# A diffusion backbone on one core: the next GEMM's first two tiles on scaled x, root and shift put on their results

## The reference

```
y = x * rsqrt(mean(x * x, axis=features) + 1e-6) * w
h = y * (1 + scale) + shift            # scale, shift from c (latent) or c_ctx (context)
layer 0: x += g1 * retention(h);        h2 = norm2(x); x += g2 * conv_ffn(h2)
layer 1: x += g1 * neighbourhood(h);    h2 = norm2(x); x += g2 * conv_ffn(h2)   # latent only from here
conv_ffn(h) = (silu(a) * g) @ w_down,   a, g = split(conv3(h @ w_up) + b),      hidden 2 x 2816
out = rmsnorm(x) * w
```

## Time and profile before

| | |
|---|---|
| time, median of 3 runs | 2078.77 us (2076.61 to 2079.49) |
| profiled execution | 2078.47 us, its span 2076.4 us |
| TensorE busy | 1982.3 us, 95% |
| VectorE, ScalarE, GpSimd busy | 65%, 36%, 5% |
| mean granted TensorE clock | 0.979 |
| DMA | 186.39 MB, 90 GB/s |

### The profile page before, as it was taken

How to read it: one execution, slowest core, us unless ns; L and a number is a source line. 1 busy time by engine, 2 the same in 40 slices (tenths; PEclk the granted TensorE clock), 3 DMA queues, 4 the chain that set the end, 5 groups by cost and what they waited for, 6 DMA issues and landing times.

```text
span 2076.4 us, 29858 instructions
## 1 busy us (share of the span) xinstructions
PE 1982.3 (95%) x10452; PEld 1687.3 (81%) x10452; DVE 1342.3 (65%) x2251; ACT 755.6 (36%) x1281; POOL 97.1 (5%) x162
## 2 busy tenths in 40 slices
PE   5999999999999889999999999899999889999997
PEld 4878888888888778888888887688888768788785
DVE  7866635735745677766664667777877667557375
ACT  4423223223313344312321233456556444333232
POOL 0000000000000000000000000311111000000000
PEclk8999999999999989999999999899999989999999
DMA  7221311321221112233224334211111222223222
GB/s 291 90 83 62 112 61 52 106 68 62 92 81 61 61 59 93 91 132 105 97 101 132 101 101 152 89 46 42 56 45 35 92 71 94 98 91 101 91 91 101
DMA packets 51256, 186.39 MB, mean 90 GB/s; under 512 B 5680, under 2 KB 5680, under 8 KB 51184
## 3 DMA queue, kind: packets, MB, share of 16 engines
q1 hardware_dynamic: 37744, 136.73, 19.4%
q0 software_dynamic: 13440, 48.63, 7.0%
HBM read 181.15 MB, written 4.19 MB: 89 GB/s over the span
## 4 chain that ended last, share of the span: by engine, by line
PE 83%; DVE 9%; issue 4%; ACT 3%; DMA 1%; DVEq 0%; SPq 0%; ACTq 0%
PE acc L393 58%; PE o_ps L483 3%; PE o_ps L518 3%; PE acc L606 3%; PE acc L483 2%; PE o_ps L649 2%; PE acc L664 2%; PE acc L505 2%; PE acc L448 2%; PE o_ps L664 2%; DVE pt_lo L1625 1%; PE acc L639 1%; PE o_ps L434 1%; PE acc L699 1%; DVE w_lo L1169 1%
## 5 line engine op out<-in xcount | busy, mean ns | idle before, releaser
L804 ACT ACTIVATE w_hi<-raw 128x1024 fp32r<-128x1024 f32 x232 | 245.2, 1057 | 597.5 <-PE acc L393 477.6
L1169 DVE TENSOR_TENSOR w_lo<-raw,w_hi 128x1024 fp32r<-128x1024 f32 x232 | 284.2, 1225 | 275.4 <-ACT w_hi L804 273.9
L393 PE MATMUL acc<-h_hi,w_hi 128*128 128x512 f32 x1520 | 437.5, 351 | 4.9 <-DVE w_lo L1169 3.4
L393 PE MATMUL acc<-h_hi,w_lo 128*128 128x512 f32 x1520 | 434.5, 349 | 0.0
L393 PE MATMUL acc<-h_lo,w_hi 128*128 128x512 f32 x1520 | 434.1, 349 | 0.0
L393 PEld LDWEIGHTS acc<-h_hi,w_hi 128*128 128x128 f32 x1520 | 245.2, 188 | 44.4 <-ACT u L990 4.2
L393 PEld LDWEIGHTS acc<-h_lo,w_hi 128*128 128x128 f32 x1520 | 245.0, 188 | 39.6
L393 PEld LDWEIGHTS acc<-h_hi,w_lo 128*128 128x128 f32 x1520 | 243.9, 188 | 38.7
L1336 DVE SCALAR_TENSOR_TENSOR x<-acc,mod,x 128x512 f32<-128x512 f32 (+3 forms) x136 | 81.9, 637 | 145.1 <-PE acc L393 135.7
L393 PE MATMUL acc<-act_hi,w_lo 128*128 128x512 f32 (+1 forms) x396 | 119.8, 356 | 0.0
L393 PE MATMUL acc<-act_hi,w_hi 128*128 128x512 f32 (+1 forms) x396 | 119.5, 356 | 0.0
(11 more groups left out here) (231 smaller groups left out, 3520.5 us busy)
## 6 DMA issues: line engine op xcount, KB each, us to landing
raw<-in_weights_dram SPq DMA_DIRECT2D x232, 512.0 KB, 3.3
ada_raw<-in_ada_dram POOLq DMA_DIRECT2D x80, 512.0 KB, 3.6
ada_start<-in_ada_first_dram SPq DMA_DIRECT2D x8, 1024.0 KB, 18.3
x<-in_x_in_dram SPq DMA_DIRECT2D x4, 768.0 KB, 7.0
park_dram<-x POOLq DMA_DIRECT2D x1, 2048.0 KB, 8.1
rel<-in_bias_dram POOLq DMA_DIRECT2D x16, 128.0 KB, 2.4
x<-park_dram POOLq DMA_DIRECT2D x2, 1024.0 KB, 6.6
out_dram<-x SPq DMA_DIRECT2D x8, 256.0 KB, 2.1
```

The source lines that it names most:

```text
L393: mm = nc.tensor.matmul(tile[:, c0:c0 + cn], wt[:, b * P:(b + 1) * P], mv[:, n, c0:c0 + cn], start=(n == 0 and m == 0), stop=(n == last an ...
L804: nc.scalar.activation(w_hi[i][:, :], raw[i][:, :], ACT.Copy).then_inc(hi_split, 1)
L1169: nc.vector.tensor_tensor(w_lo[i][:, :], raw[i][:, :], w_hi[i][:, :].bitcast(F32), ALU.subtract)\
```

## The change

Each of the three norms now works like this. VectorE makes A ahead of the output tiles (`raw_scale`), and the shift as two more columns of h in high and low part, which is why `h_hi` and `h_lo` are two columns wider. As each block of x is complete, ScalarE writes the high part of x times A into `h_hi` (`raw_high`) and VectorE the low part into `h_lo` (`raw_low`). TensorE goes from the last output tile to two tiles on these (`raw_two`), the sums of squares and the spread between their blocks; the last block's squares aren't added by VectorE but summed by a second set of matmuls (`final_sums`). The norm then runs behind: `norm` overwrites a block of `h_hi` once both tiles have read it (`raw_used`). VectorE multiplies the two results by the spread root (`take_raw`), and ScalarE adds the two shift columns as a bias: into `u` for the FFN, into the values and the high part of the keys for the attention.

The root chain is shorter everywhere: the reciprocal alone is made by VectorE, and `spread_roots` multiplies its broadcast column by the identity, 128 tokens at a time. In the mid norms ScalarE copies the spread from PSUM to `ss`, from which VectorE reads it. The first turn of each FFN's first loop and its last group of output tiles are written out instead of looped.

```diff
@@ TensorE
             def spread_roots(parts):
-                pe.wait_ge(diag_done, diags.up())
-                for c0, cn, _ in parts:
-                    mm = nc.tensor.matmul(spread[:, c0:c0 + cn], ones[:, :], ss[:, c0:c0 + cn], start=True, stop=True)
+                pe.wait_ge(roots_ready, diags.up())
+                for t in range((parts[-1][0] + parts[-1][1]) // P):
+                    mm = nc.tensor.matmul(spread[:, t * P:(t + 1) * P], rms[:, t:t + 1].to_broadcast([P, P]), ident,
+                                          start=True, stop=True)
...
+            def final_sums(width):
+                pe.wait_ge(sq_added, squares_added.up(KC) - 1)
+                for t in range(width // P):
+                    mm = nc.tensor.matmul(sums[:, 2 * t:2 * t + 2], ss[:, t * P:(t + 1) * P], ones[:, 0:2],
+                                          start=(t == 0), stop=False)
+                mm.then_inc(sq_added, 1)
+                pe.wait_ge(sq_done, squares_added.now())
+                for t in range(width // P):
+                    mm = nc.tensor.matmul(sums[:, 2 * t:2 * t + 2], S[1][:, t * P:(t + 1) * P], ones[:, 0:2],
+                                          start=False, stop=(t == width // P - 1))
+                mm.then_inc(sums_done, 1)
...
+            def raw_two(width, tiles=None):
...
+                def blocks(j, n0, n1):
+                    tile, w = jobs[j]
+                    for n in range(n0, n1):
+                        if j == 0:
+                            pe.wait_ge(h_lo_done, first + n + 1)
+                        for m, (wt, mv) in enumerate(((w[0], h_hi), (w[0], h_lo), (w[1], h_hi))):
+                            for c0, cn, o0 in RAW_PARTS[width]:
+                                mm = nc.tensor.matmul(tile[:, o0:o0 + cn], wt[:, n * P:(n + 1) * P], mv[:, n, c0:c0 + cn],
+                                                      start=(n == 0 and m == 0), stop=(n == KC - 1 and m == 2))
...
+                        elif j == 1:
+                            mm.then_inc(raw_used, 1)
+                pe.wait_ge(shift_cols, raw_turns.up(2))
+                open_job()
+                blocks(0, 0, 4)
+                final_sums(width)
+                blocks(0, 4, 5)
+                open_job()
+                blocks(1, 0, 1)
+                blocks(0, 5, 6)
+                blocks(1, 1, 2)
+                spread_roots(PARTS if width == TOK else PARTS[:1])
+                blocks(0, 6, 7)
+                blocks(1, 2, 3)
+                blocks(0, 7, 8)
+                blocks(1, 3, 8)
@@ ffn
-                        project_two(parts, ready)
-                    with turns(pe, size - first, A.steps(2) + [(chunk, 2)]):
+                        raw_two(parts[-1][0] + parts[-1][1])
+                        project(h_hi, h_lo, parts, h_ready(h_split.now()))
+                        project(h_hi, h_lo, parts)
+                    with turns(pe, size - 2 * first, A.steps(2) + [(chunk, 2)]):
@@ before the attention
-            token_sums(KC, TOK)
-            spread_roots(PARTS)
-            project_two(PARTS, h_ready(h_split.now()), (1, 0))
-            part(queries(), 0, KC)
+            raw_two(TOK, (1, 0))
+            part(queries(), 0, KC, h_ready(h_split.now()))
@@ ScalarE
+            def raw_high(m, parts, by_column=False):
+                for c0, cn, c in parts:
...
+                    ins = nc.scalar.activation(o, a, ACT.Identity, scale=norm_a[:, m, c:c + 1])
...
+            def norm(layer, shift, parts, tiles, finish):
                 root(D, width)
+                act.wait_ge(spread_done, roots.now())
+                nc.scalar.activation(ss[:, 0:width], spread[:, 0:width], ACT.Copy).then_inc(spread_copied, 1)
...
                 for k in range(KC):
                     act.wait_ge(norm_t, normed.up())
+                    if k < KC - 1:
+                        act.wait_ge(raw_used, used + k + 1)
...
+                    if k in (2, 5):
...
+                        act.wait_ge(acc_full, full)
+                        split()
+                    if k in (3, 7):
...
+                        finish(k // 4)
@@ VectorE
-                step(nc.vector.reciprocal(rms[:, 0:t], rms[:, 0:t]))
-                nc.vector.tensor_tensor(ss[:, 0:width].rearrange("p (t q) -> p t q", q=P),
-                                        ident.rearrange("p (t q) -> p t q", t=1).to_broadcast([P, t, P]),
-                                        rms[:, 0:t].rearrange("p (t q) -> p t q", q=1).to_broadcast([P, t, P]),
-                                        ALU.mult).then_inc(diag_done, 1)
+                nc.vector.reciprocal(rms[:, 0:t], rms[:, 0:t]).then_inc(roots_ready, 1)
...
+            def raw_low(m, parts, by_column=False):
+                dve.wait_ge(h_hi_done, h_hi_made.up())
...
+                    ins = nc.vector.scalar_tensor_tensor(o, a, norm_a[:, m, c:c + 1], b, ALU.mult, ALU.subtract)
...
+                def take_raw(j):
...
+                    nc.vector.tensor_copy(lift[:, 2 * j:2 * j + 2], tile[:, TOK:TOK + 2])
...
+                        ins = nc.vector.tensor_tensor(o, a, b, ALU.mult)
+                    ins.then_inc(acc_taken[i], 1)
+                    split()
...
+                    if k == 1:
+                        take_raw(0)
                 h_split.up(2)
+                take_raw(1)
@@ out_projection(final): the same in the last group of FFN 0 and in the attention's output
+                    raw_scale(0, 2, 24, PARTS)
...
+                    if final and m < KC - 1:
+                        add_square(m % 2, TOK)
                     if final:
-                        add_square(m % 2, TOK)
+                        raw_low(m, PARTS)
```

More of the change, by code:

```diff
@@ L999, in ffn @@
-                    last = n == len(GROUPS) - 1
-                    for m in range(2):
-                        t, after = wait_after()
-                        split()
-                        if last:
-                            final_square(t, after, 0, m, width)
-                    pairs = 2 if ends and last else 3
-                    with turns(act, pairs, A.steps(2) + [(raws[0], 16), (raws[1], 16), (squares_added, 2 * last)]) as i:
-                        for m in range(2):
-                            t, after = wait_after()
-                            split()
-                            if last:
-                                final_square(t, after, 2 * i + 2, m, width)
@@ L1012, in ffn @@
-                    if pairs == 2:
-                        for m in range(2):
-                            t, after = wait_after()
-                            final_square(t, after, 6, m, width)
+                    act.wait_ge(conv_done, convs.now() + (layer + 2))
+                    w = width + (len(parts) > 1)
+                    nc.scalar.activation(S[2][:, 0:w], S[0][:, 0:w], ACT.Silu).then_inc(silu_done, 1)
+                    convs.up(2)
+                    act.wait_ge(act_mul, products.up())
@@ L1303, in norm @@
+            def norm(layer, shift, parts, by_column, tiles=None):
+                width = TOK if len(parts) > 1 else LAT
                 one_over(width)
-                rooted()
+                dve.wait_ge(spread_copied, scales.now() + 1)
                 def scaled(k):
                     for c0, cn, c in parts:
-                        o, a, b = (z[:, c0:c0 + cn] for z in (S[2 + k % 2], x[:, k, :], spread))
+                        o, a, b = (z[:, c0:c0 + cn] for z in (S[2 + k % 2], x[:, k, :], ss))
@@ L1505, in ffn, with outputs @@
                 f0 = 0
+                def outputs(m, loads, row, conds):
+                    add_gated(m, layer, 40, parts)
+                    if not ends or not last or m < KC - 2:
+                        split()
+                    if last and m < KC - 1:
+                        add_square(m % 2, w_all)
+                    if last and not ends:
+                        raw_low(m, parts, True)
+                    if loads:
+                        ada_step(row, waste, conds)
                 for n, size in enumerate(GROUPS):
@@ L1540, in ffn @@
                     own_done()
-                    pairs = 2 if ends and n == 2 else 3
                     last = n == len(GROUPS) - 1
```

270 lines of the change are left out of this document (174 added, 96 removed).

## The result

| | us, median | runs |
|---|---|---|
| before | 2078.43 | 4 (2076.61 to 2079.49) |
| after | 2099.74 | 4 (2091.76 to 2100.21) |

The ratio is 1.0094 (95% interval 1.0069 to 1.0120). Measured again beside other runs of before (`after_again`) it is 1.0107 (1.0091 to 1.0122). The profiled execution took 2100.0 us, its span 2098.1, 21.7 more than before.

A forecast was written before the change was run, and what follows sets the result against it. TensorE bounds the kernel (83% of the wait chain), with idle at the norms; +1.0 + 2.0 + 1.2 - 1.0 - 1.2 - 0.3 = +1.7 on 2078.47, median 0.3 above: 2080.4 us, range 2076 to 2085 (8 in 10: 2071.5 to 2088).

The forecast's parts named there:

- The wider rows of h (3%): Rival, 3%: rows 770 long start blocks off the old raster; at 1% on these matmuls, over 10 us slower.
- The norm before the attention, +2.0: Norm before attention: nothing gained, since keys wait for the whole norm; lost clock, partly under softmax, +2.0 (0 to 3.5).
- the start of the norm goes from 10.9 to 13.8: Before the attention: the norm starts 13.8 us after the projection's end instead of 10.9.
- The clock behind the sums: 15.1 for 13.8: First mid norm: 8 blocks and both sums 11.2, spread to 12.9, copy to 13.8, when the norm starts; before, 10.7.
- VectorE can't feed the tiles (25%): Rival, 25%: scaled x's low part in output tiles makes split weights late, TensorE stands; adds 7 us, 2087.
- First mid norm, +1.0: Before the first FFN: fifth tile 1.8 us earlier, but a moved 5.5 us wait costs 2.8 of clock: +1.0.
- Second mid norm, +1.2: Later weight split in attention's output projection +2.2, earlier fifth tile -3.6, lost clock +2.6: +1.2 (-1.5 to +2.5).
- Start -1.0: At the kernel's start, the 768-wide diagonal product leaves a VectorE chain: -1.0, or 0 if a transfer sets the pace.
- End -1.2: At the kernel's end, the diagonal product in a 1.30 wait and an addition of squares go: -1.2.
- Heads -0.3: In the four heads, the wait of 0.18 goes and the spread becomes six pieces, twelve passes: -0.3 together.
- The spread's weight loads are hidden: Denied by a rival, 7%: unhidden loads make passes up to 0.22 instead of 0.117 at seven places; likely +6, 2086.
- The copy of the spread: ScalarE's new copy of the spread from PSUM to SBUF adds 0.8 us and saves nothing, against a skill rule.

The follow-up runs named there:

- pad128: The kernel before with 128 unused bytes behind h_lo, so every later array lies 128 bytes further on, rows still 768: 2089.26 us, 1.0063.
- after_laid: The changed kernel, same operations, streamed arrays laid at 128 modulo 256 bytes, rows of h 768 apart in heads and second FFN, 770 between: 2085.37 us, 1.0040.
- best: swap_laid with the last sums and the spread placed earlier among the blocks of the raw tiles, at all three norms: 2073.55 us, 0.9987.
- swap_laid: after_laid with the raw tiles before the attention going to accumulators 0 and 1 instead of 1 and 0: 2077.94 us, 1.0012.
- swap: The changed kernel with the raw tiles before the attention going to accumulators 0 and 1 instead of 1 and 0: 2091.72 us, 1.0073.
- before_laid: The kernel before with the rows of act in the second FFN 160 bytes further on, at 128 modulo 256: 2074.22 us, 0.9990.
- pitch: TensorE alone, all else left out: matmuls and pairs timed at 24 SBUF placements; 226.7 ns per 512-column matmul at before's placement, 232.3 at after's.
- best2: best with act and vg at 224 modulo 256 where pairs read them, at 128 in the second FFN: 2068.93 us, 0.9969.
- h768: The changed kernel with rows of h 768 long again, shift columns in arrays of their own, read by additional 2-column matmuls: 2097.66 us, 1.0100.

## Why the prediction was wrong, step by step

- **The wider rows of h (3%), or rather what lies behind them: about 12 us.** The main miss, and the step that failed is the sentence "two columns more per matmul are nothing". The unchanged stretches lose 2.2, 3.8 and 6.1 us. The cause is where rows lie relative to the weights modulo 256 bytes. The two columns moved the weights, which is the greater part (pad128 alone makes before 13 us longer; in after_laid the heads and the second FFN lose nothing), and they took the blocks of h off the weights' place, which is the 3.5 us left in the first FFN. The prediction had the size ("over 10 us") and named a rival, with a cause that is half right: it looked at the rows alone, and gave it a chance with no row behind it.
- **The norm before the attention, +2.0: measured +9.5** (56.0 less the 46.5 of before; +6.6 in after_again), or +10.8 with the feed of the last tiles; in best +1.7 with that feed. The step that failed is "the start of the norm goes from 10.9 to 13.8", which let the raw tile start at once. It took account of VectorE's load per tile, but not of which accumulator the tile opens in. The price in after is 4.03 of wait and 3.0 of half clock behind it (5.91 us at 0.50), 7.0 together. That is what swap_laid takes back (the norm's first product from 22.1 to 15.1); after_again has the wait and some 3 us less behind it.
- **The clock behind the sums: 15.1 for 13.8.** Where the raw tile does start at once, at the first mid norm in after and before the attention in swap_laid, the norm's first product comes 15.1 us behind the projection. The spread is due 11.2 behind it by the forecast and starts 12.7 behind, because the clock falls behind the passes of the two sums:

```profile
727.60:731.01 3.41, 3.41 (x13) 2.93 (x13) 0.23 (x7) 0.38 (x3) 0.00 (x0) 0.50 0.25 99
```

  That is 1.7 us which the forecast has nowhere. In swap, whose program is the same up to there, the clock stays at 1.00 through this stretch, the spread starts 11.2 behind and the first product 13.5: the forecast's steps were right but for the clock.
- **VectorE can't feed the tiles (25%): true in one place.** Splits 126 to 132 fall 2.1 to 2.5 us behind in every kernel with the new low part by column; pad128, without it, loses nothing there. At the first projection the splits come 2.6 us later too (60 to 64), but TensorE does not wait for them.
- **First mid norm, +1.0: measured +0.1** (after and after_laid, splits 60 to 70), or +1.3 against the same stretch of before_laid, so it is right within the scatter. The fifth tile's start was right to 0.1 us, but by luck in part: the norm began 1.3 later than forecast, and from the first convolution to the fifth tile's split it took 11.7, not 12.5. Its wait was 4.23 for 5.5; the clock took 1.7 (5.42 us at 0.69), not 2.8:

```profile
771.58:777.00 5.42, 5.42 (x22) 4.69 (x23) 5.31 (x8) 1.26 (x3) 0.00 (x0) 0.69 0.31 97
```

- **Second mid norm, +1.2: measured -0.1 in after and after_again, and -0.7 in after_laid**, within the scatter of 1.7 seen there. The wait for the split in the output projection is 4.29, against 2.37 + 2.2 forecast. The fifth tile starts 33.2 behind the projection (1733.60 less 1700.43), for 34.9, and its wait is 2.28, for 3.8:

```profile
1680.87 0.79 PE L741 MATMUL acc<-no_hi,w_hi 128*128 128x512 f32 x1 [4.29 <-DVE w_lo L1260]
1733.60 0.50 PE L397 MATMUL acc<-h_hi,w_hi 128*128 128x512 f32 x1 [2.28 <-DVE w_lo L1260]
```

  The clock behind the two waits:

```profile
1680.87:1686.75 5.88, 5.88 (x14) 4.62 (x15) 4.63 (x6) 2.29 (x4) 0.00 (x0) 0.50 0.46 153
1733.60:1738.00 4.40, 4.40 (x12) 3.48 (x13) 4.26 (x7) 1.16 (x3) 0.00 (x0) 0.61 0.40 133
```

  So behind the fifth tile's wait 1.7 is lost, not 2.6. The longer wait in the output projection costs 2.9 of clock, where in before the shorter one cost 1.7 (1660.21 to 1663.60 at 0.51); these 1.2 the forecast had at nothing.
- **Start -1.0: -1.2 measured** at the first split, some of it given back by split 6 in after, not in after_again, so that is scatter. **End -1.2: -1.9** (23.6 at the last split, 21.7 at the end). **Heads -0.3:** not to be read: splits 12 to 60 give -0.2, -1.8 and +0.1 in after_laid, swap_laid and best, which have the same program there. The spread's weight loads are hidden: twelve passes in 1.50 above, before's four wide ones in 1.56. **The copy of the spread** saves nothing, as forecast: the 512-wide product of the norm takes 751 ns out of `ss`, 747 out of PSUM before.
- **Keys**: the low part in eight pieces took 5.53, not the 4.4 assumed.
- A few of the forecast's sums are rounded up by 0.1 to 0.2 (12.9 + 0.8 is 13.7, and 36.8 + 12.5 is 49.3), which changes nothing.

The three norms by themselves were forecast at +4.2. With the layout taken out, after_laid shows +0.1, +11.0 with the feed of the tiles, and -0.7.

## What to carry to other kernels

Before costing a change's instructions, list which arrays it moves: an allocator that packs tensors makes any new size a change to every array behind it, and a test that adds bytes and nothing else (pad128) shows it in one run. When a step is moved up to follow another directly, check the resource that it opens (accumulator, slot) as well as the data: who used it last, and when is it given back. And a loss seen in stretches that the change doesn't touch is to be explained first.

## What the runs showed of the hardware

- The pitch of fp32r matmuls depends on where the moving rows and the weights lie, modulo 256 bytes: in `pitch`, 512 columns take 226.7 to 227.3 ns where they agree, 231.7 to 233.3 in the placements tried where they don't.
- Pairs of 512 and 256 columns on the same weights take 353.1 to 353.3 or 346.7 ns where they agree (two levels, in one execution of before), and 349.2 to 353.1 elsewhere: 350.1 and 350.2 with the rows 96 bytes past the weights' place, 353.1 with the rows 32 or 64 short of it. So alignment is right for single matmuls. For pairs, rows 96 bytes on were the better choice in best2, and its runs scatter less.
- Two columns in a matmul of their own, between others, took 0.107 us of TensorE at full clock (h768).
- The clock does not fall alike in every execution. Behind the two sets of sums at the first mid norm it went to 0.50 for 3.41 us in after and stayed at 1.00 in swap, with the same program up to there.
